# A block of two layers and attention: where the convolution taps stand among the key steps of the input projection

## The chip, the cores and the metric

The kernel runs on one core of a Trainium2 chip. The metric is the device time of one execution in microseconds (us); it was measured in three runs, and one more execution was profiled.

## The reference

The program computes two models one after the other on 512 tokens with 256 context tokens, all of width 1024: a two-layer block (a convolution branch beside a recurrence over 8 heads, then a SwiGLU network), and a block with attention and 32 experts. What matters here is the start of a layer, for x and for the context alike:

```python
ux = modulate(rmsnorm(x, norm1_g[l]), sh1, sc1) @ w_in[l]   # 23 column tiles of 128 or fewer
val, gate = jnp.split(ux[..., :1024], 2, axis=-1)           # tiles 0 to 7
z = dwconv(val * jax.nn.sigmoid(gate), conv_w) + conv_b     # 31 taps for each of 512 channels
u = dwconv(ux[..., 1024:], shift_w)                         # 3 taps, tiles 8 to 23
r, k, v, w_lo, a_lo, g_lo = jnp.split(u, ...)
kk = k * k_k
kk = kk / jnp.maximum(jnp.sqrt(jnp.sum(kk * kk, axis=-1, keepdims=True)), 1e-12)   # per head
```

## The kernel before

Each engine's program is written out by hand, in its own order, and the engines hold each other by semaphores. In the input projection of a layer (`input_projection`, one function of that name on each engine) they all walk through the same list, `input_steps`. It has the steps "product" n for n = 0 to 23, one column tile of the projection each (P0 to P23 below); behind each product from 16 on a "key" step, two for each of the four key tiles t (first half and second half); and "mod" and "turn" steps, small products for the next modulation. The order from P16 on is P16, key 0a, P17, key 0b, P18, key 1a, turn, mods, P19, key 1b, mods, P20, key 2a, P21, key 2b, turn, mods, P22, key 3a, P23, key 3b, mods, turn.

A product on TensorE (PE) is 24 matmuls over the 512 tokens and 24 over the context (three for each of 8 tiles, since operands are split into a high and a low part). It writes one of four pairs of PSUM banks, taken in turn by every product, head sum, mod and turn, so that one of these waits until the bank pair of the fourth before it has been read.

For P8 to P23, ScalarE (ACT) copies the product out of PSUM into `tmp` and, times the middle shift tap, into `work` (`raw_column`, L2420 to L2425). It then writes the high part of the weights two units ahead (`in_high`, L2648), for which the weight slot must have been loaded. VectorE (DVE) adds the other two shift taps (`token_shift`, L1622 and L1624) and writes the low part of the weights (`in_low`, L1663). Weights come in slots of 1024 KB through a ring of four; a slot is given free by the first matmul after its last use.

The first half of a key step for tile t is on DVE `start_key` (it scales tile t-1 by the finished norm, `scale_key` L1639, and multiplies the key tile, L1647) and on ACT the square of the result into the tile `rs` (L2463). The second half is on PE the head sum of `rs` (a product with `head_sum`, 128x512 and 128x256), on DVE `key_sum` (L1655, back into `rs`), and on ACT `key_norm`: logarithm (L2439) and exponential (L2443), each with a load of its table.

The convolution is on DVE alone, as 31 taps for each of four channel tiles: `conv_taps` issues the taps `first` to `last` of the table `CONV_ORDER`, one instruction each (L1610 the first of a tile, L1608 the others). A tap k on channel tile c waits for tap k-1 on the same tile. The last four taps stand at the end of the projection, behind the last `scale_key`. The others fill in between: 36 (`EARLY_TAPS`) behind products 3 to 7, and 84 inside `token_shift` of products 8 to 19, 7 in each. In the code of DVE these 7 come before the key step that follows the product:

```python
                late = len(CONV_ORDER) - 4 - EARLY_TAPS
                first, last = (EARLY_TAPS + late * min(m, TAP_COLUMNS) // TAP_COLUMNS for m in (n, n + 1))
                conv_taps(layer, first, last)
```

Of the kernel before, what the change touches and what calls it, by code (L numbers as in the profile page):

```python
# [20 lines left out]
TAPS = 31  # L21
# [50 lines left out]

def conv_order():

    order = [(k, c) for k in range(EARLY_TAPS // 2) for c in (0, 1)]
    order += [(k, c) for k in range(EARLY_TAPS // 2) for c in (2, 3)]
    order += [(k, c) for k in range(EARLY_TAPS // 2, TAPS) for c in range(4)]
    return [(k, c, order.index((k - 1, c)) if k else None) for k, c in order]


def raw_tile(n):


    return n - 8 if n < 16 else n - 4 if n < 20 else n - 12


def mod_groups(layer):

    return ([(0, q) for q in range(2, 6)] + [(1, 0), (1, 1)], [(1, q) for q in range(2, 6)] + [(2, 0), (2, 1)])[layer]


def in_unit(n):

    return n if n < 17 else n - 1
# [12 lines left out]
def input_steps(layer):  # L107

    n, turn = 0, None
    for slot in range(12):  # L110
        for h in range(((2,) * 8 + (3, 1) + (2,) * 2)[slot]):
            yield "product", n, h
            if n >= 16:
                yield "key", (n - 16) // 2, n % 2
            n += 1
        if turn:
            yield "turn", turn, None
            turn = None
        for i in range(2 * slot, 2 * slot + 2):
            yield "mod", mod_groups(layer)[i // 4], i % 4  # L120
        if i % 4 == 3:
            turn = mod_groups(layer)[i // 4]
    yield "turn", turn, None


EARLY_TAPS, TAP_COLUMNS = 36, 12
CONV_ORDER = conv_order()


# [101 lines left out]
def build(nc, ins, out):  # L231

    ctx = ExitStack()
    with ctx:
# [9 lines left out]
        def sem(name):  # L244
            return ctx.enter_context(nc.semaphore(name))
# [111 lines left out]
        def V(name, i=0, n=None):  # L357
            o, c = VOFF[name]
            return vec[:, o + i:o + i + (n or 1)]
# [19 lines left out]
        freed = {o: sem(f"product_read_{o}") for o in ("dve", "act")}  # L379
# [142 lines left out]
        def xs(t):  # L522
            return t[..., XO:XO + SEQ]

        def cs(t):
            return t[..., 0:CTX]
# [26 lines left out]
        def parts(with_ctx):  # L553

            return ((xs, 0), (cs, 1)) if with_ctx else ((xs, 0),)

        def grid(t, layer):

            return t.rearrange("p (c r) -> p r c", r=GRID_R) if layer == 1 else t.rearrange("p (r c) -> p r c", c=GRID_W)

        def natural(t):
            return t.rearrange("p (r c) -> p r c", c=GRID_W)

        def halves(j):

            return psum[:, 2 * j, :], psum[:, 2 * j + 1, 0:CTX]
# [956 lines left out]
        def _(dve):  # L1523
            w = Counts()
            banks = Results()
# [63 lines left out]
            def gated_value(layer, c):  # L1589
                j = banks.pair("dve")  # L1590
                dve.wait_ge(ready["dve"], banks.n["dve"])
                px, pc = halves(j)
                dve.wait_ge(freed["act"], gate_read[c])
                z = zp[:, c, GAP:GAP + W]
                tt(grid(xs(z), layer), natural(px), grid(xs(kk[:, c, :]), layer), ALU.mult)
                tt(cs(z), pc, cs(kk[:, c, :]), ALU.mult).then_inc(freed["dve"], 1)
                if c % 2:
                    dve.wait_ge(freed["dve"], banks.n["dve"])

            def conv_taps(layer, first, last):  # L1600

                for i in range(first, last):
                    k, c, before = CONV_ORDER[i]
                    a = 0 if layer == 0 else XO
                    src, acc, wt = zp[:, c, k + a:k + W], scr[:, c, a:W], V(f"conv_w{layer}", c * TAPS + k)
                    if k:
                        dve.wait_ge(conv_tap, w.seen[conv_tap] - i + before + 1)
                        ins = stt(ht[:, c, a:W] if k == TAPS - 1 else acc, src, wt, acc, ALU.mult, ALU.add)  # L1608
                    else:
                        ins = ts(acc, src, wt, V(f"conv_b{layer}", c), ALU.mult, ALU.add)  # L1610
                    ins.then_inc(conv_tap, 1)
                    w.skip(conv_tap)

            def token_shift(layer, n):
                banks.pair("act")
                dve.wait_ge(freed["act"], banks.n["act"])
                m = raw_tile(n + 8)
                rows = 64 if m in (12, 13) else 32 if m == 15 else P
                dst = (rkv[:, m, :] if m < 12 else lo[:, m - 12, :])[0:rows]
                src = tmp[0:rows, n % 2, :]  # L1620
                tap = lambda k: V(f"shift_w{layer}", 3 * m + k)[0:rows]
                stt(dst, src[:, 0:W], tap(0), dst, ALU.mult, ALU.add).then_inc(dve_chain, 1)  # L1622
                dve.wait_ge(dve_chain, w.next(dve_chain))
                stt(dst, src[:, 2:2 + W], tap(2), dst, ALU.mult, ALU.add).then_inc(raw_used, 1)  # L1624
                dve.wait_ge(raw_used, w.next(raw_used))
                u = in_unit(n + 8) + 2
                if n + 8 != 16 and u < 23:
                    in_low(layer, u)
                late = len(CONV_ORDER) - 4 - EARLY_TAPS
                first, last = (EARLY_TAPS + late * min(m, TAP_COLUMNS) // TAP_COLUMNS for m in (n, n + 1))  # L1630
                conv_taps(layer, first, last)

            gate_read = {}

            def scale_key(t):

                dve.wait_ge(gstd, w.next(gstd))
                for f, b in parts(True):
                    ins = tt(f(kk[:, t, :]), f(kk[:, t, :]), f(rs), ALU.mult)  # L1639
                ins.then_inc(dve_chain, 1)  # L1640
                dve.wait_ge(dve_chain, w.next(dve_chain))
# [17 lines left out]
            def in_low(layer, u):  # L1659

                dve.wait_ge(in_w_high, w.next(in_w_high))
                raw, low = in_weights(layer, u)[1]
                tt(low, raw, w_high[:, u % 2].bitcast(F32), ALU.subtract).then_inc(in_w_low, 1)  # L1663

            def input_projection(layer):
                for step, n, h in input_steps(layer):
                    if step == "key":
                        (key_sum if h else start_key)(layer, n)
                    elif step != "product":
                        banks.pair("act")  # L1670
                    elif n in (0, 1, 4, 5):
                        banks.pair("act")
                        gate_read[n // 4 * 2 + n % 2] = banks.n["act"]
                        in_low(layer, n + 2)
                        if n >= 3:
                            conv_taps(layer, EARLY_TAPS * (n - 3) // 5, EARLY_TAPS * (n - 2) // 5)
                    elif n < 8:
                        gated_value(layer, n // 4 * 2 + n % 2)
                        in_low(layer, n + 2)
                        if n >= 3:  # L1680
                            conv_taps(layer, EARLY_TAPS * (n - 3) // 5, EARLY_TAPS * (n - 2) // 5)
                    else:
                        token_shift(layer, n - 8)
                        if n == 19:
                            dve.memset(lo[64:65, 0:2, :], 1.0).then_inc(shifted, 1)
                scale_key(3)
                conv_taps(layer, len(CONV_ORDER) - 4, len(CONV_ORDER))
                dve.wait_ge(conv_tap, w.seen[conv_tap])
                dve.memset(mark, 0.0).then_inc(conv_out, 1)
                dve.wait_ge(conv_out, w.next(conv_out))  # L1690
# [345 lines left out]
            for layer in range(2):  # L2036
# [7 lines left out]
                if layer == 0:  # L2044
# [4 lines left out]
                    modulation(0, 0, 2)  # L2049
                norm(0, layer, True)  # L2050
                input_projection(layer)
                modulation(layer, 2, 6)
                modulation(layer + 1, 0, 2)
# [1017 lines left out]
```

## Time and profile before

| what | us |
|---|---|
| median of three runs | 4542.56 |
| lowest and highest of them | 4535.45, 4549.70 |
| the profiled execution's own time | 4540.72 |
| its span, first to last instruction | 4538.5 |
| input projection of layer 0, from P2 to the last tap | 85 to 344 |
| the same of layer 1 | 1501 to 1757 |
| busy share of the span: PE, DVE, ACT | 92%, 55%, 35% |

The profile is one execution, so its rows add up to 4540.72 us and not to the median. All times within it are from the span's start. The granted clock is given as a share of TensorE's full speed.

### The profile page before, as it was taken

What the parts mean: (1) busy time and instruction counts of PE and PEld (TensorE: products, weight loads), DVE (VectorE), ACT (ScalarE), POOL (GpSimd) and SP (SyncE); (2) the same over time, 40 slices, a digit from 0 to 9 for tenths busy, and PEclk for the clock granted to TensorE, in tenths of its full rate; (3) what the DMA queues carried; (4) which work ended last, traced back from release to release, by engine and by line L of the source; (5) the groups of instructions that cost most, each with busy time, mean ns of one, the idle gap of its engine ahead of it and who ended that gap; (6) DMA issues with size and microseconds to landing.
All of it is one profiled execution on the core that took longest, in us unless ns stands there. A gap on an engine that the chain in (4) does not pass through costs nothing.

```text
span 4538.5 us, 84941 instructions
## 1 busy us (share of the span) xinstructions
PE 4155.1 (92%) x37041; PEld 3207.8 (71%) x37041; DVE 2516.0 (55%) x3175; ACT 1568.7 (35%) x1923; POOL 118.8 (3%) x114
## 2 busy tenths in 40 slices
PE   6977998999999987999899969788699999999996
PEld 4857997588887866999488655443477777777774
DVE  4956775332222674776443320463477777777774
ACT  3243223100021334322200221253356666666662
POOL 0000000000000000000000000000200000000000
PEclk9988999999999998999999989899699999999997
DMA  6430000111122331000222225000499999999994
GB/s 246 154 116 12 4 4 31 56 65 57 65 68 86 145 135 61 4 4 4 84 94 98 96 73 188 25 1 29 170 336 353 356 354 352 359 356 355 352 357 143
DMA packets 115974, 663.46 MB, mean 146 GB/s; under 512 B 13632, under 2 KB 14656, under 8 KB 57696
## 3 DMA queue, kind: packets, MB, share of 16 engines
q1 hardware_dynamic: 102496, 610.68, 36.0%
q0 software_dynamic: 13168, 48.10, 3.9%
q8 instruction: 261, 4.28, 0.4%
q14 instruction: 49, 0.40, 0.0%
HBM read 637.62 MB, written 30.68 MB: 147 GB/s over the span
## 4 chain that ended last, share of the span: by engine, by line
PE 82%; DVE 11%; ACT 4%; DMA 2%; issue 2%; POOL 0%; SPq 0%; DVEq 0%; ACTq 0%; POOLq 0%
PE psum L791 54%; PE psum L1430 16%; PE psum L1456 5%; PE psum L1447 4%; DVE work L1608 2%; DVE xt L1812 1%; PE psum L1423 1%; DVE work L2138 1%; DMA ring<-stream 1%; PE psum L1404 1%; PE psum L1414 1%; DVE ring_parts L1663 0%; PE psum L1316 0%; POOL places L729 0%; DVE work L1624 0%
## 5 line engine op out<-in xcount | busy, mean ns | idle before, releaser
L791 PE MATMUL psum<-work 64*64 64x64 f32 (+3 forms) x12552 | 631.6, 239 | 66.2 <-ACT work L2747 21.8
L791 PE MATMUL psum<-ht_parts,ahead_parts 128*128 128x512 f32 (+1 forms) x2016 | 673.4, 350 | 0.6 <-DVE ht_parts L2005 0.6
L791 PEld LDWEIGHTS psum<-work 64*64 64x64 f32 (+2 forms) x12552 | 508.5, 138 | 145.2 <-issue 58.7
L791 PE MATMUL psum<-work_parts,ring_parts 128*128 128x512 f32 x1344 | 481.7, 359 | 0.0
L791 PE MATMUL psum<-work_parts,ahead_parts 128*128 128x512 f32 x1248 | 432.7, 359 | 10.3 <-ACT work_parts L2400 10.0
L791 PEld LDWEIGHTS psum<-ht_parts,ahead_parts 128*128 128x128 f32 (+1 forms) x2016 | 368.9, 186 | 60.7 <-issue 1.5
L791 PE MATMUL psum<-ht,ring 128*128 128x512 f32 (+1 forms) x832 | 315.4, 540 | 8.1 <-DVE ht L2154 6.1
L791 PEld LDWEIGHTS psum<-work_parts,ring_parts 128*128 128x128 f32 x1344 | 254.5, 189 | 40.0
L791 PE MATMUL psum<-xt_parts,ahead_parts 128*128 128x512 f32 (+5 forms) x768 | 265.1, 347 | 18.8 <-ACT xt_parts L2400 13.0
L791 PEld LDWEIGHTS psum<-ht,ring 128*128 128x128 f32 x832 | 157.8, 191 | 163.7 <-issue 150.9
L1430 PE MATMUL psum<-work_parts 128*128 128x512 f32 x1024 | 273.4, 393 | 0.0
L791 PEld LDWEIGHTS psum<-work_parts,ahead_parts 128*128 128x128 f32 x1248 | 234.5, 189 | 48.0 <-issue 11.5
L791 PE MATMUL psum<-xt_parts,ring_parts 128*128 128x512 f32 (+5 forms) x768 | 261.2, 342 | 0.0
L2242 DVE TENSOR_TENSOR ring_parts<-ring,work_parts 128x2048 fp32r<-128x2048 f32 x97 | 221.9, 2287 | 68.3 <-ACT work_parts L2809 68.3
L2809 ACT ACTIVATE work_parts<-ring 128x2048 fp32r<-128x2048 f32 x97 | 185.9, 1917 | 131.2 <-DMA ring<-w_in 120.7
L2242 DVE TENSOR_TENSOR ht_parts<-ht,work_parts 128x2048 fp32r<-128x2048 f32 x94 | 215.2, 2290 | 24.7 <-ACT work_parts L2809 24.5
L1430 PEld LDWEIGHTS psum<-work_parts 128*128 128x128 f32 x1024 | 192.6, 188 | 44.9 <-DVE ring_parts L2242 0.3
L2524 ACT ACTIVATE work<-psum 128x512 f32<-128x512 f32 x168 | 100.3, 597 | 344.7 <-PE psum L791 344.6
L1456 PE MATMUL psum<-ring,work 128*128 128x512 f32 x496 | 217.9, 592 | 0.0
L2601 ACT ACTIVATE work<-psum 128x512 f32<-128x512 f32 x44 | 26.3, 598 | 547.3 <-PE psum L791 547.3
L1430 PE MATMUL psum<-ring_parts,work_parts 128*128 128x512 f32 x768 | 211.3, 396 | 0.0
L1941 DVE SCALAR_TENSOR_TENSOR xt<-psum,mod,xt 128x512 f32<-128x512 f32 x40 | 32.8, 820 | 321.0 <-PE psum L791 321.0
(324 smaller groups left out, 7066.2 us busy)
## 6 DMA issues: line engine op xcount, KB each, us to landing
ring<-stream SPq DMA_DIRECT2D x192, 1024.0 KB, 4.9
ring<-w_in SPq DMA_DIRECT2D x192, 1024.0 KB, 6.7
ht<-w_in SPq DMA_DIRECT2D x64, 1024.0 KB, 6.4
ht<-w_out SPq DMA_DIRECT2D x64, 1024.0 KB, 7.4
ring<-w_out SPq DMA_DIRECT2D x64, 1024.0 KB, 7.0
xt<-xt_rows POOLq DMA_DIRECT2D x2, 3132.0 KB, 10.5
xt_rows<-xt POOLq DMA_DIRECT2D x1, 3132.0 KB, 14.3
xt_rows<-xt POOLq DMA_DIRECT2D x8, 391.5 KB, 3.2
```

The source lines that it names most:

```text
L791: mm = pe.matmul(*args, **kwargs)
L1404: mm = flush(pe.transpose(psum[:, 4 + k // 4, P * (k % 4):P * (k % 4) + P], x_tok[:, P * k:P * k + P], ident))
L1414: mm = flush(pe.transpose(psum[:, 4 + k // 4, P * (k % 4):P * (k % 4) + P], act[:, P * k:P * k + P], ident))
L1423: flush(pe.matmul(psum[:, b, :], one_hot, b_parts[:, 512 * b:512 * b + 512], start=True, stop=False))
L1430: mm = flush(pe.matmul(psum[:, b, :], x[:, k, :], wt[:, 512 * b:512 * b + 512], start=False, stop=(k == KT - 1 and x is x_low)))
L1447: flush(pe.matmul(psum[:, 6 + c, :], lhs[:, a], wt[:, f, 512 * c:512 * c + 512], start=(h == 0 and f == 0 and k == 0), stop=False))
L1456: mm = flush(pe.matmul(psum[:, 6 + c, :], e_act_high[:, P * (2 * h + f):P * (2 * h + f) + P], wt[:, f, 512 * c:512 * c + 512], start=False ...
L1608: ins = stt(ht[:, c, a:W] if k == TAPS - 1 else acc, src, wt, acc, ALU.mult, ALU.add)
L1812: ins = tt(dst[i % 2][:, g], ps, tri[:, g].to_broadcast([P, 4, 2, C]), ALU.mult)
L2242: tt(low_slots[k], raw_slots[k], highs[j % HIGHS].bitcast(F32), ALU.subtract).then_inc(low_ready, 1)
L2524: fn(dst, result(name, n, bank), ACT.Copy).then_inc(read_of[name], 1)
L2809: fn(highs[j % HIGHS], raw_slots[n % EXPERT_RING], ACT.Copy).then_inc(high_ready, 1)
```

## The change

Of the 124 taps of a layer none is added or left out; what moves is where they stand in the order of DVE. `TAPS_AT` says how many taps stand behind each place: indices 0 to 15 are the products 0 to 15, indices 16 to 22 the key steps 0a to 3a, each now behind the key step and not before it. So 5 taps stand behind product 2, 7 behind each of products 3 to 15, 3 behind each of key 0a, 0b, 1a and 1b, 4 behind each of key 2a, 2b and 3a, and as before 4 at the end. In `CONV_ORDER` the first ten taps are five of channel tile 0 and then five of tile 1, and the third and fourth tile begin at tap 40. Since taps of a tile now stand behind its gated value for tile 0 and 2 too, `gated_value` waits for its own result for every tile.

```diff
 def conv_order():
 
-    order = [(k, c) for k in range(EARLY_TAPS // 2) for c in (0, 1)]
+    first = [(k, 0) for k in range(5)] + [(k, 1) for k in range(5)]
+    order = first + [(k, c) for k in range(5, EARLY_TAPS // 2) for c in (0, 1)]
...
-EARLY_TAPS, TAP_COLUMNS = 36, 12
+EARLY_TAPS = 40
+TAPS_AT = [0, 0, 5] + [7] * 13 + [3] * 4 + [4] * 3 + [0]
...
-                if c % 2:
-                    dve.wait_ge(freed["dve"], banks.n["dve"])
+                dve.wait_ge(freed["dve"], banks.n["dve"])
...
             def input_projection(layer):
+                def taps_at(n):
+                    conv_taps(layer, sum(TAPS_AT[:n]), sum(TAPS_AT[:n + 1]))
+
                 for step, n, h in input_steps(layer):
                     if step == "key":
                         (key_sum if h else start_key)(layer, n)
-                    elif step != "product":
+                        taps_at(16 + 2 * n + h)
+                        continue
+                    if step != "product":
...
+                    if n < 16:
+                        taps_at(n)
```

PE, ACT, GpSimd and the DMA queues issue the same instructions in the same order as before. On DVE, the following is its order in layer 0 from the token shift of P16 (the rows 64x783) to `key_sum` of key 0b (rs<-psum), before. The rows work<-work,vec 128x783 x7 are taps, the TENSOR_SCALAR between them is `start_key`, and ring_parts is `in_low`.

```order
L1622 SCALAR_TENSOR_TENSOR work<-work,vec 64x783
L1624 SCALAR_TENSOR_TENSOR work<-work,vec 64x783
L1608 SCALAR_TENSOR_TENSOR work<-work,vec 128x783 x7
L1647 TENSOR_SCALAR work<-work,vec 128x783
L1622 SCALAR_TENSOR_TENSOR work<-work,vec 64x783
L1624 SCALAR_TENSOR_TENSOR work<-work,vec 64x783
L1663 TENSOR_TENSOR ring_parts<-ring,ahead_parts 128x8x128
L1608 SCALAR_TENSOR_TENSOR work<-work,vec 128x783 x7
L1655 TENSOR_SCALAR rs<-psum 128x512
```

The same stretch of DVE in the changed kernel, where the key multiplication is at L1646, the key sum at L1654 and a tap at L1610:

```order
L1624 SCALAR_TENSOR_TENSOR work<-work,vec 64x783
L1626 SCALAR_TENSOR_TENSOR work<-work,vec 64x783
L1646 TENSOR_SCALAR work<-work,vec 128x783
L1610 SCALAR_TENSOR_TENSOR work<-work,vec 128x783 x3
L1624 SCALAR_TENSOR_TENSOR work<-work,vec 64x783
L1626 SCALAR_TENSOR_TENSOR work<-work,vec 64x783
L1662 TENSOR_TENSOR ring_parts<-ring,ahead_parts 128x8x128
L1654 TENSOR_SCALAR rs<-psum 128x512
L1654 TENSOR_SCALAR rs<-psum 128x256
L1610 SCALAR_TENSOR_TENSOR work<-work,vec 128x783 x3
```

Seven taps before each half of key 0 have become three behind each. Near the start of the projection, DVE now has taps between the gated values of tiles 0 and 1 (work<-psum,work), which stood right behind `in_low` before:

```order
L1662 TENSOR_TENSOR ring_parts<-ring,ahead_parts 128x8x128
L1612 TENSOR_SCALAR work<-work,vec 128x783
L1610 SCALAR_TENSOR_TENSOR work<-work,vec 128x783 x4
L1598 TENSOR_TENSOR work<-psum,work 128x512
L1599 TENSOR_TENSOR work<-psum,work 128x256
```

The first two rows behind `in_low` are the five taps of channel tile 0 that moved forward.

## Rows read from the trace of the kernel before

**Rows 1.** Busy time in four stretches; PEclk is the granted clock.

```profile
84.00:239.00 155.00, 155.00 (x1057) 127.71 (x1050) 129.68 (x138) 38.46 (x76) 0.00 (x0) 1.00 0.43 163
239.00:340.00 101.00, 77.51 (x470) 57.14 (x468) 55.46 (x66) 44.00 (x75) 0.00 (x0) 0.87 0.32 115
1500.00:1655.00 155.00, 154.57 (x1051) 127.31 (x1044) 106.72 (x138) 48.37 (x76) 0.00 (x0) 1.00 0.43 163
1655.00:1753.00 98.00, 77.24 (x471) 57.22 (x469) 47.20 (x63) 49.23 (x73) 0.00 (x0) 0.88 0.33 119
```

**Rows 2.** Chain of work, layer 0: start us, us, what.

```profile
236.11 6.71 DVE work L1608 x7
...
262.55 4.80 DMA ring<-stream
...
284.62 6.62 DVE work L1608 x7
```

**Rows 3.** Chain of work, layer 1.

```profile
1652.37 4.73 DVE work L1608 x7
```

**Rows 4.** PE, instructions in order of time, layer 0; in brackets idle before, releaser.

```profile
244.29 2.93 PE L791 MATMUL psum<-rs,con 128*128 128x512 f32 x4 [4.77 <-ACT rs L2463]
...
261.98 0.39 PE L791 MATMUL psum<-xt_parts,ahead_parts 128*32 128x512 f32 x1 [2.01 <-ACT work L2425]
...
279.14 2.90 PE L791 MATMUL psum<-rs,con 128*128 128x512 f32 x4 [7.04 <-ACT mod L2363]
...
305.51 1.66 PE L791 MATMUL psum<-rs,con 128*128 128x512 f32 x4 [2.67 <-ACT rs L2463]
306.97 3.41 PE L791 MATMUL psum<-con,work 128*128 128x2 f32 x16
310.31 3.56 PE L791 MATMUL psum<-ring,work 128*32 128x256 f32 x32
313.80 0.50 PE L791 MATMUL psum<-xt_parts,ahead_parts 128*128 128x512 f32 x1
...
330.79 0.59 PE L791 MATMUL psum<-rs,con 128*128 128x512 f32 x1
```

**Rows 5.** PE in order of time, layer 1, the same places.

```profile
1658.57 1.22 PE L791 MATMUL psum<-rs,con 128*128 128x512 f32 x1 [2.78 <-ACT rs L2463]
...
1743.87 0.59 PE L791 MATMUL psum<-rs,con 128*128 128x512 f32 x1
```

**Rows 6.** DVE in order of time, layer 0: gated value 1, a column, a key step, P22.

```profile
102.15 0.69 DVE L1595 TENSOR_TENSOR work<-psum,work 128x512 f32<-128x512 f32 x1 [5.70 <-PE psum L791]
...
184.53 1.03 DVE L1622 SCALAR_TENSOR_TENSOR work<-work,vec 128x783 f32<-128x783 f32 x1
...
186.66 1.23 DVE L1663 TENSOR_TENSOR ring_parts<-ring,ahead_parts 128x1024 fp32r<-128x1024 f32 x1
187.81 6.70 DVE L1608 SCALAR_TENSOR_TENSOR work<-work,vec 128x783 f32<-128x783 f32 x7
...
276.34 1.02 DVE L1639 TENSOR_TENSOR work<-work,rs 128x512 f32<-128x512 f32 x2
277.40 0.63 DVE L1647 TENSOR_SCALAR work<-work,vec 128x783 f32<-128x783 f32 x1
...
324.44 1.04 DVE L1622 SCALAR_TENSOR_TENSOR work<-work,vec 128x783 f32<-128x783 f32 x1 [12.88 <-ACT work L2425]
```

**Rows 7.** ACT in order of time, layer 0: key norm, raw column, high weights, square.

```profile
256.96 0.94 ACT L2439 ACTIVATE rs<-rs 128x512 f32<-128x512 f32 x2 [8.79 <-DVE rs L1655]
...
260.05 0.58 ACT L2420 ACTIVATE work<-psum 128x512 f32<-128x512 f32 x1
...
261.36 0.48 ACT L2425 ACTIVATE work<-psum,vec 128x256 f32<-128x256 f32 x1
267.43 1.06 ACT L2648 ACTIVATE ahead_parts<-ring 128x1024 fp32r<-128x1024 f32 x1 [5.59 <-DMA ring<-stream]
278.06 0.85 ACT L2463 ACTIVATE rs<-work 128x783 f32<-128x783 f32 x1 [9.58 <-DVE work L1647]
```

More of the change, by code:

```diff
@@ L123, in input_steps @@
     yield "turn", turn, None
-EARLY_TAPS, TAP_COLUMNS = 36, 12
+EARLY_TAPS = 40
+TAPS_AT = [0, 0, 5] + [7] * 13 + [3] * 4 + [4] * 3 + [0]
+assert sum(TAPS_AT) == 4 * TAPS - 4 and sum(TAPS_AT[:8]) == EARLY_TAPS
 CONV_ORDER = conv_order()
@@ L1628, in token_shift @@
                     in_low(layer, u)
-                late = len(CONV_ORDER) - 4 - EARLY_TAPS
-                first, last = (EARLY_TAPS + late * min(m, TAP_COLUMNS) // TAP_COLUMNS for m in (n, n + 1))
-                conv_taps(layer, first, last)
             gate_read = {}
@@ L1668, in input_projection @@
                         (key_sum if h else start_key)(layer, n)
-                    elif step != "product":
+                        taps_at(16 + 2 * n + h)
+                        continue
+                    if step != "product":
                         banks.pair("act")
-                    elif n in (0, 1, 4, 5):
+                        continue
+                    if n in (0, 1, 4, 5):
                         banks.pair("act")
@@ L1674, in input_projection @@
                         in_low(layer, n + 2)
-                        if n >= 3:
-                            conv_taps(layer, EARLY_TAPS * (n - 3) // 5, EARLY_TAPS * (n - 2) // 5)
                     elif n < 8:
@@ L1679, in input_projection @@
                         in_low(layer, n + 2)
-                        if n >= 3:
-                            conv_taps(layer, EARLY_TAPS * (n - 3) // 5, EARLY_TAPS * (n - 2) // 5)
                     else:
```

## The prediction

> **What bounds the kernel now.** I read the two stretches that the change touches, in four windows first. Up to P17 PE is busy all the time at the full clock, 155 of 155 us in layer 0 and 154.57 in layer 1; in the stretch of the key steps it is busy 77.51 of 101 us and 77.24 of 98, and the granted clock falls to 0.87 and 0.88 [rows 1]. So PE loses about 23 and 21 us there by waiting, and something more by its clock. The chain of waits then says who makes it wait. In layer 0 it runs through four groups of seven taps, 6.6 to 6.7 us each, between the token shifts and the key steps (the first and the last are shown), and through one load of a weight slot [rows 2]; in layer 1 through four such groups of 4.6 to 4.7 us (the first is shown) [rows 3]. PE's own rows show where it lands: 4.77 us idle before the head sum of key 0, 2.01 before P19, 7.04 before the head sum of key 1, 2.67 before that of key 2 [rows 4].
>
> The mechanism is plain in the code and in these rows. PE is in order, so the head sum of a key blocks the product behind it. It needs ACT's square, which needs `start_key`, and that stands behind 7 taps on DVE. Likewise `key_sum` stands behind 7 taps, ACT's key norm waits for it, and behind the key norm stands ACT's raw column of P18, whose bank P19 needs. P19's first matmul frees the slot whose load the next high weights need.
>
> **What one step costs.** From the rows of DVE: token shift 2.13 us (184.53 to 186.66), low weights 1.15, a tap 0.95 (seven in 6.6); scale 1.06 and key multiplication 0.64 [rows 6]. In layer 1 a tap is 0.67 (4.7 for seven) [rows 3]. From ACT: square 0.8, key norm 3.1 (256.96 to 260.05), raw column 1.8, high weights 1.07 [rows 7]. From PE at full clock: two products in 16.99 us (313.80 to 330.79), so 8.5 each; a head sum 1.45 (305.51 to 306.97) [rows 4]. The turn and the mods, at the lower clock 3.34 and 3.49 in these rows, I take at 1.85 and 1.9, half of that and a little over. The load of a slot ends 5.4 us after the matmul that frees the last one (261.98 to 267.35) [rows 2, 4].
>
> **Layer 0, replayed with the taps behind the key steps.** Up to P16 nothing on the path changes: DVE's column of 9.9 us stays as it was, with seven taps.
>
> Key 0: the token shift of P16 ends at 236.1, where now the seven taps begin [rows 2]. The key multiplication follows at once, the square is ready near 237.7, and P17 ends on PE only at 239.5 (244.29 less its idle of 4.77) [rows 4]. The head sum starts then: 4.8 us earlier, no gap. It ends at 240.9, P18 at 249.4, turn and mods at 253.2.
>
> P19: raw column of P17 239.5 to 241.4, then three taps are long done (239.6), token shift and low weights until 244.7, `key_sum` until 245.8, key norm until 248.9. The raw column of P18 starts with the end of P18 at 249.4 and is read out at 251.3, before PE comes to P19 at 253.2. The gap of 2.01 is gone; P19 is 8.8 us earlier than 261.98.
>
> Key 1: P19 starts at 253.2, its freed slot is loaded at 258.6, high weights 259.7, low weights 260.9, scale and multiplication 262.6, square 263.4, the turn's copy 0.2, so the head sum starts at 263.8. PE was done with P19 at 261.7: a gap of 2.1 stays where 7.04 was. 15.3 us earlier than 279.14.
>
> P20 and P21 run from 267.2 to 284.2. `key_sum` of key 1 comes at 272, long before P21's bank is needed. Square 2 is ready near 283.5 (raw column of P20 277.6, token shift, low weights, scale, multiplication, square: 5.8 more), so key 2 has no gap: head sum 284.2, 21.3 earlier than 305.51. Turn and mods until 289.5. P22 needs the bank of this head sum: raw column of P21 until 286.1, four taps done at 286.5, token shift and low weights 289.8, `key_sum` 290.9. P22 starts at 291.0, a new gap of 1.5, where it started at 313.80: 22.8 earlier. P22 and P23 take 17, and nothing holds key 3. What is behind the head sum of key 3 (330.79) is as before. **Layer 0 gains 22.8 us if PE keeps its full clock.**
>
> **Layer 1,** the same way with taps of 0.67, the raw column near 2.6 and P17 ending at 1655.8 (1658.57 less 2.78) [rows 5]: head sum 0 at once (2.78 earlier), P19 at 1669.4, head sum 1 at 1680.0 after a gap of 2, P20 at 1683.4, head sum 2 at 1701.1 after a gap of 0.7, P22 at 1708.1 after a gap of 1.9, head sum 3 at 1725.1 in place of 1743.87 [rows 5]. **It gains 18.8.** As a bound from the other side, the 28 taps taken out of the chain are 26.6 us in layer 0 and 18.7 in layer 1 [rows 2, 3].
>
> **The clock.** The head sum after the gap of 4.77 took 2.4 (244.29 to the next product at 246.7) and not 1.45, the turn and the mods after the gap of 2.67 took 6.8 and not 3.7 [rows 4], and the stretch was granted 0.87 [rows 1]. In the replay gaps of 0.7 to 2.1 stay, two in layer 0 and three in layer 1. If none is followed by a spell at 1.2 GHz, the gain is 41.6 as summed; if each is followed by one that costs as much as in these rows, 1 to 3 us, it is 31 to 37. The row before P19 has a gap of that size, 2.01, and the sum can't say which way it goes, so I take off 2 us for each layer. **Sum: 41.6 - 4 = 37.6 us.**
>
> On this the Trainium skill has a rule: TensorE: Matmul & The Clock Gate, in the part on the clock gate, says that the throttled state is the default and that activity releases it. By that rule only the long gaps would cost clock, and since they go the gain would be near the 41.6. This trace agrees for the gap of 4.77 and shows the full clock through the 155 busy us ahead of it.
>
> **Edits costed at nothing.** The 24 taps that now stand behind key steps are hidden by waits of DVE for ACT's raw columns: in the replay DVE still waits before every token shift from P17 on but that of P21, which the four taps before it delay by 0.4. Without that cover they would cost 24 x 0.95 + 24 x 0.67 = 39 us. The five taps behind P2 take 4.9 us, within the 5.70 that DVE idles before the gated value of tile 1 [rows 6]; taps of one tile in a row wait for each other, which a pair of dependent instructions shows as 1.07 in place of 0.95 apart (184.53 to 186.66 for two) [rows 6], so 0.5 more for these five: still inside. Were they late by all of it, `in_low` of P5 would have a whole product in hand. The additional wait in `gated_value` is for DVE's own last instruction and is 0.1 us at most in the same pair, twice a layer. All other engines issue the same order. The convolution's last four taps and all behind them follow the key norm of key 3 as before.
>
> **The rivals.** (a) The taps behind keys 2a, 2b and 3a come onto the path. Before, there were none from P20 on, so this part is new load: 12 x 0.95 + 12 x 0.67 = 19.4 us. DVE's idle there speaks against it, 12.88 us before the token shift of P22 [rows 6], though it shrinks by the taps. It would leave 18 us: 4524. (b) All 24 are on the path: then only four taps of each layer are saved, 3.8 + 2.7 = 6.5 us, 4536, which counts as no change. Key 0 speaks against it in the replay: its three taps end at 239.6, and the raw column that DVE waits for next is ready at 241.4. (c) The gain is real but is given back, because what follows waits for something that does not move, the spill of xt or the weights of the recurrence. 4543. Against it: the queues move 115 GB/s here against 163 ahead [rows 1], and each load is released by a matmul that itself moves. (d) Slower: PE is busy without a break for longer, and its clock is granted at the lower level through the key stretches. Eight products of 8.5 us in each layer would cost 136 us more, which gives 4542.6 - 41.6 + 136 = 4637; it decides from 41 us of PE work at half speed on. The 155 us of unbroken work at 1.00 [rows 1] speak against it.
>
> **How the numbers follow.** The chances: forecast 0.80, (a) 0.09, (b) 0.04, (c) 0.04, (d) 0.03. The profiled execution was 4540.72, the median of the three runs 4542.56; the gain is the same for both: 4540.7 - 37.6 = 4503.1, and against the median 4542.6 - 37.6 = 4505.0, which I predict. The forecast's own range is a gain of 31 to 44, 4499 to 4512. The range given is 4495 to 4525: it takes in (a), a run-to-run spread of some us (the three runs lie 14 apart) and, below, a gain of the 28 taps in both layers (45.3). Under 0.3%, 13.6 us, a measurement of this kernel can't tell a difference. Faster by more: forecast and (a), 0.89; within: (b) and (c), 0.08; slower: 0.03.
>
> **What would show it.** In the changed trace: no idle of PE before head sum 0 and P19; 2 us before head sum 1 on the high weights' load; none or little before head sum 2; 1 to 2 us before P22, on `key_sum`; head sum 3 near 308 and 1725 - 22.8 = 1702; the granted clock of the key stretches over 0.93; no taps in the chain between a token shift and a key step. The prediction is wrong if taps stand in the chain still, if PE's gap before head sum 1 is more than 4 us, or if the recurrence begins no earlier.

## The result and the profile after

The changed kernel takes 4509.99 us (median of four runs, 4508.09 to 4518.09) against 4542.8 before (four runs: the three of the table above and the profiled one): 0.9931 of the time, 95% interval 0.9912 to 0.9951. That is 32.8 us faster, where 37.6 were forecast; the time lies in the range given. The profiled execution has a span of 4505.9 us, 32.6 less than that of before.

Busy time of the changed kernel, in the first stretch of [rows 1], then in its key steps of layer 0 and of layer 1 (columns as there):

```profile
84.00:239.00 155.00, 155.00 (x1044) 127.85 (x1043) 133.45 (x141) 38.96 (x75) 0.00 (x0) 1.00 0.43 162
239.00:322.00 83.00, 71.21 (x476) 55.18 (x474) 55.37 (x64) 42.50 (x73) 0.00 (x0) 0.94 0.41 147
...
1639.00:1723.00 84.00, 71.18 (x475) 54.17 (x472) 46.23 (x61) 49.39 (x74) 0.00 (x0) 0.93 0.39 138
```

The key stretches are 83 and 84 us long in place of 101 and 98. PE idles 12 to 13 us in them and not 21 to 24, and the granted clock is 0.94 and 0.93 in place of 0.87 and 0.88 [rows 1].

PE of the changed kernel in order of time, layer 0, which answers to [rows 4]:

```profile
237.48 1.45 PE L794 MATMUL psum<-rs,con 128*128 128x512 f32 x4
238.58 0.58 PE L794 MATMUL psum<-xt_parts,ahead_parts 128*128 128x512 f32 x1
...
263.31 2.15 PE L794 MATMUL psum<-rs,con 128*128 128x512 f32 x4 [3.87 <-ACT mod L2366]
265.40 2.94 PE L794 MATMUL psum<-ring,work 128*32 128x256 f32 x32
268.27 0.49 PE L794 MATMUL psum<-xt_parts,ahead_parts 128*128 128x512 f32 x1
...
292.06 0.46 PE L794 MATMUL psum<-xt_parts,ahead_parts 128*128 128x512 f32 x1 [1.82 <-DVE rs L1654]
...
309.00 0.59 PE L794 MATMUL psum<-rs,con 128*128 128x512 f32 x1
```

The head sum of key 0 follows P17 with no gap. P19 has none either. Before the head sum of key 1 a gap of 3.87 us is left of 7.04, and a new one of 1.82 stands before P22. The program began this stretch 1.84 us earlier by chance of its start-up (gated value 0 on DVE at 91.85, at 93.69 before), so head sum 3, at 309.00 and 330.79 before [rows 4], is 19.95 us nearer to that point. The same in layer 1, its PE waits of the key stretch:

```profile
PE psum L794 <- ACT work L2360: 6.5, 1, 6.5
PE psum L794 <- ACT mod L2366: 4.1, 1, 4.1
PE psum L794 <- DVE rs L1654: 1.8, 1, 1.8
PE psum L794 <- ACT rs L2466: 0.3, 1, 0.3
```

The first of these stands behind head sum 3 and was there before; the second is the gap before head sum 1, the third that before P22.

The chain of work of the changed kernel where that gap ends, layer 0:

```profile
251.44 6.69 DMA ring<-stream
...
258.22 1.07 ACT ahead_parts L2651
...
259.38 1.23 DVE ring_parts L1662
260.61 0.95 DVE work L1638 x2
...
261.58 0.64 DVE work L1646
...
263.00 0.17 ACT mod L2366
```

No tap stands in this piece. What it waits for is the load of the weight slot, 6.69 us and not 4.80 [rows 2], and the two weight steps behind it.

Taps are not gone from the chain altogether. In layer 0 it runs, ahead of P22, through the four taps behind key 2a; in layer 1 no taps stand in it from key 0 to P22. The same chain, layer 0:

```profile
283.83 3.87 DVE work L1610 x4
...
287.70 0.96 DVE work L1624
...
290.89 1.03 DVE rs L1654 x2
...
292.06 17.13 PE psum L794 x96
```

DVE of the changed kernel at the two places where its taps come closest to something (the four taps behind key 2a, and the first five):

```profile
95.49 4.24 DVE L1610 SCALAR_TENSOR_TENSOR work<-work,vec 128x783 f32<-128x783 f32 x4
100.26 0.69 DVE L1598 TENSOR_TENSOR work<-psum,work 128x512 f32<-128x512 f32 x1 [0.53 <-PE psum L794]
...
283.83 3.87 DVE L1610 SCALAR_TENSOR_TENSOR work<-work,vec 128x783 f32<-128x783 f32 x4
287.62 1.03 DVE L1624 SCALAR_TENSOR_TENSOR work<-work,vec 128x783 f32<-128x783 f32 x1
```

The first five are done 0.53 us before the gated value of tile 1 is wanted. The four behind key 2a end as the token shift of P21 begins, without idle between them.

**Where the time is.** Five pieces of the two traces give the 32.6 us of the span. The start-up gave 1.84, layer 0 19.95. From the end of layer 0's taps (344.38 before, 322.53 after) to the first low weights of layer 1 (1499.95 and 1483.99) the changed kernel takes 5.9 us more. Layer 1, from there to head sum 3 (1743.87 and 1712.67), gives 15.24, and the rest of the program 1.4. The 5.9 us are the part that the prediction had not foreseen. The first and the last piece are chance as far as the traces show: the second trace of before (before_again, below) spends 3.6 us less in the rest of the program than the first (2791.1 and 2794.7), with the same kernel. So the two layers are surer than the total.

### The profile page after: what moved, and what is told of

Its sections match the earlier page's. It is cut to its first block, busy times and chain, and to the rows that moved or that the text cites. A ratio compares the mean times of both kernels' runs of the same rounds, so it can differ in the third digit from the quotient of the medians.

```text
span 4505.9 us, 84943 instructions
## 1 busy us (share of the span) xinstructions
PE 4146.4 (92%) x37041; PEld 3204.2 (71%) x37041; DVE 2518.4 (56%) x3175; ACT 1570.2 (35%) x1923; POOL 118.8 (3%) x114
## 4 chain that ended last, share of the span: by engine, by line
PE 85%; DVE 8%; ACT 3%; DMA 2%; issue 1%; POOL 0%; SPq 0%; DVEq 0%; ACTq 0%; POOLq 0%
PE psum L794 57%; PE psum L1433 16%; PE psum L1459 5%; PE psum L1450 4%; DVE xt L1815 1%; DVE work L2141 1%; PE psum L1426 1%; DMA ring<-stream 1%; PE psum L1407 1%; PE psum L1417 1%; POOL places L732 0%; PE psum L1319 0%; ACT work L2750 0%; DMA sum_rows<-work 0%; DVE ht L1561 0%
## 5 line engine op out<-in xcount | busy, mean ns | idle before, releaser
L1944 DVE SCALAR_TENSOR_TENSOR xt<-psum,mod,xt 128x512 f32<-128x512 f32 x40 | 32.8, 820 | 323.0 <-PE psum L794 323.0
```

## The experiments

All edits are against the changed kernel, but for `before_again`. The table has, for each profiled execution, the stretch of layer 0 (gated value 0 to head sum 3), the stretch between the layers (behind the last tap of layer 0, in `delayed` behind its fills, to the first low weights of layer 1), PE's busy time in it, how much of this is at the lower clock (1.2 GHz), and the stretch of layer 1 (first low weights to head sum 3), in us. The ratios are to runs of the kernel before that were made along with each kernel, whose medians were 4542.8 (for changed), 4539.19 (again, behind_only, spread_ahead, no_key_taps) and 4541.18 (the others):

| kernel | median | ratio to before, 95% | layer 0 | between | PE busy between | of it at the lower clock | layer 1 |
|---|---|---|---|---|---|---|---|
| before | 4542.8 | | 237.10 | 1155.6 | 1091.1 | 34.1 | 243.92 |
| before_again | 4540.99 | 1.0002 (0.9991 to 1.0012) | 237.20 | 1155.5 | 1091.1 | 34.1 | 244.02 |
| changed | 4509.99 | 0.9931 (0.9912 to 0.9951) | 217.15 | 1161.5 | 1097.3 | 47.4 | 228.68 |
| again | 4509.11 | 0.993 (0.9913 to 0.9946) | 217.53 | 1161.3 | 1097.0 | 47.5 | 228.51 |
| behind_only | 4513.76 | 0.9942 (0.9925 to 0.9958) | 218.96 | 1161.3 | 1099.4 | 51.5 | 227.89 |
| spread_ahead | 4530.07 | 0.998 (0.9969 to 0.999) | 233.89 | 1156.0 | 1091.4 | 34.2 | 239.11 |
| no_key_taps | 4505.90 | 0.9933 (0.9916 to 0.9949) | 217.06 | 1159.1 | 1094.2 | 39.7 | 228.27 |
| delayed | 4512.09 | 0.9936 (0.9922 to 0.9949) | 217.25 | 1158.2 | 1094.1 | 40.9 | 227.75 |
| late_weights | 4497.12 | 0.9907 (0.9892 to 0.9922) | 213.04 | 1155.5 | 1091.1 | 34.3 | 222.80 |
| late_weights_2 | 4492.62 | 0.9895 (0.9881 to 0.9908) | 210.07 | 1161.6 | 1097.3 | 48.0 | 221.65 |

### behind_only: the place alone

```diff
-    first = [(k, 0) for k in range(5)] + [(k, 1) for k in range(5)]
-    order = first + [(k, c) for k in range(5, EARLY_TAPS // 2) for c in (0, 1)]
+    order = [(k, c) for k in range(EARLY_TAPS // 2) for c in (0, 1)]
...
-EARLY_TAPS = 40
-TAPS_AT = [0, 0, 5] + [7] * 13 + [3] * 4 + [4] * 3 + [0]
+EARLY_TAPS = 36
+TAPS_AT = [0, 0, 0, 7, 7, 7, 7, 8] + [7] * 8 + [7] * 4 + [0] * 4
```

> Only the place is changed: the counts and the order of taps are those of before (36 by product 7, seven with each of products 8 to 19), but for products 16 to 19 the seven stand behind the key step and not ahead of it. Theory (the place is what counts; taps behind a key step are hidden by the waits for raw columns even when there are seven): head sum 3 of layer 0 within 2 us of where the changed kernel has it, 309.0, and the time within 5 us of 4510. Rival (the spread over more key steps and the five early taps matter): seven taps behind key 0a and 0b delay the next token shift, 2 to 4 us in each of four places are lost, and the time is 4520 to 4530.

Layer 0 is 18.1 us shorter than before and layer 1 16.0, against 19.95 and 15.24 for the whole change. The median is 4513.76, 3.8 us over the changed kernel. Head sum 3 stands at 313.07, 4 us later than 309.0, where within 2 us was expected; but this execution had also begun later (gated value 0 at 94.11), and set against that point it is 1.8 us. So the place carries the gain. The spread, with the five early taps, gives 1.8 us in layer 0, where seven taps of 0.95 us behind a key step leave a gap of 1.3 before head sum 2, and nothing in layer 1, where a tap is 0.67. PE's waits of the key stretch, layer 0, of behind_only:

```profile
PE psum L793 <- ACT work L2359: 5.8, 1, 5.8
PE psum L793 <- ACT mod L2365: 3.9, 1, 3.9
PE psum L793 <- ACT rs L2465: 1.3, 1, 1.3
PE psum L793 <- DVE rs L1653: 1.1, 1, 1.1
```

### spread_ahead: the counts alone

```diff
-                        (key_sum if h else start_key)(layer, n)
                         taps_at(16 + 2 * n + h)
+                        (key_sum if h else start_key)(layer, n)
```

> The other part alone: the counts and the order of the changed kernel (5 behind product 2, 3 and 4 with the seven key steps), but the taps of a key step stand ahead of it, as before. Theory: they are on the chain, 24 in place of 28, and those of keys 2a, 2b and 3a are new there; head sum 3 of layer 0 is only 5 to 9 us earlier than 330.8, the time is 4525 to 4535. Rival (fewer taps in each place is what brings the gain): most of the gain is kept, 4512 to 4520.

Layer 0 gains 3.2 us, less than the 5 to 9 expected, and layer 1 4.8, 8.0 in all; the median is 4530.07, within the range expected and 9.1 below that of before in the same set of runs. The taps are on the chain of work again, three or four at a time, those of the keys from 2a on included (spread_ahead, layer 0):

```profile
245.53 2.84 DVE work L1610 x3
...
264.72 2.84 DVE work L1610 x3
...
290.48 3.78 DVE work L1610 x4
...
301.92 3.78 DVE work L1610 x4
...
321.09 3.87 DVE work L1610 x4
```

Three or four taps ahead of a key step cost nearly what seven did in fewer places. The rival that fewer taps in each place bring the gain is out.

### no_key_taps: what the hidden taps still cost

```diff
-TAPS_AT = [0, 0, 5] + [7] * 13 + [3] * 4 + [4] * 3 + [0]
+TAPS_AT = [0, 0, 5] + [7] * 13 + [0] * 8
+CONV_K = TAPS - 6
```

> Leaves part of the computation out: the convolution has 25 of its 31 taps, and the 24 that stood behind the key steps are gone; all else stands as in the changed kernel. Theory (they are fully hidden): the same time as the changed kernel within 3 us, head sum 3 of layer 0 near 309. Rival (they still cost, above all those behind keys 2a, 2b and 3a, where DVE's token shift of P21 follows without a wait): up to 19 us less, by 12 taps of 0.95 and 12 of 0.67.

The run leaves out six of the 31 taps of each channel tile, and with them all taps behind the key steps. Layer 0 takes 217.06 us without the taps and 217.15 with them, layer 1 228.27 and 228.68. The 24 taps, 22.8 and 16 us of work, cost 0.1 and 0.4 us, no more than two traces of the changed kernel differ by (0.4 and 0.2). The median, 4505.90 against 4509.99, is 4.1 us less where within 3 was expected; it differs by the stretch between (1159.1 against 1161.5) and by what one run differs from the next. The gap before head sum 1, 4.0 us here, isn't made by taps at all. That before P22 in layer 0 is 1.6 us in place of 1.8, so the four taps that stand in the chain there cost about 0.2 us.

### again and before_again: the 5.9 us between the layers

Both kernels unchanged, for a second trace.

> The changed kernel once more, for a second trace. Between the end of the projection of layer 0 and P2 of layer 1 the first trace of the changed kernel is 5.9 us longer than that of before (the lead is 21.85 us at the last tap and 15.96 at P2 of layer 1). Theory 1: that is the granted clock of the work in between, which differs from one execution to the next, and is no cost of the change: this stretch, 1162.8 us in the first trace of the changed kernel and 1156.9 before, will be off 1162.8 here by some us either way. Rival: it is a cost of the change (another clock phase set by the earlier arrival): the stretch will be 1162.8 again within 1 us.

> The kernel before once more, for a second trace. A second run of the changed kernel had its stretch from the last tap of layer 0 to P2 of layer 1 at 1161.3 us, as the first (1161.5), against 1155.6 in the one trace of before: my theory that this is chance from run to run has fallen. Theory now: each kernel has its own fixed length there, set by where the granted clock falls; before will have 1155.6 within 1 us. Rival: before varies, and its one trace was lucky: 1158 to 1162.

The first theory fell: the changed kernel had 1161.3 us again. The second held: before has 1155.5. In two traces of each kernel it isn't chance from run to run. The stretch between in the first trace of before (columns as in [rows 1]):

```profile
344.40:1500.00 1155.60, 1091.11 (x14448) 932.06 (x14452) 509.90 (x912) 235.57 (x400) 4.87 (x9) 0.97 0.13 44
```

The same in the first trace of the changed kernel:

```profile
322.50:1484.00 1161.50, 1097.25 (x14448) 936.83 (x14452) 509.72 (x912) 235.56 (x400) 4.87 (x9) 0.97 0.13 43
```

And in that of again:

```profile
323.50:1484.90 1161.40, 1097.04 (x14448) 937.45 (x14452) 509.80 (x912) 235.56 (x400) 4.87 (x9) 0.97 0.13 43
```

PE has the same 14448 matmuls in all of them, DVE and ACT the same busy time to 0.2 us. The matmuls alone are 6 us longer. What makes the same matmuls longer is the clock. Of PE's busy time in this stretch 34.1 us are at the lower of its two levels before, and 47.4 in the changed kernel. At half speed the 13.3 us more hold 6.7 us of full-speed work, which so costs 6.7 us more, against 6.1 measured; over all ten traces the table's two columns agree in this way within 0.8 us. An example is the end of the recurrence, where PE comes back after 11.5 us idle (at 781.43 before, at 761.48 in the changed kernel). Before, its clock is at the lower level until 784.70 and at the full one in the output projection behind it:

```profile
774.46:784.70 10.24, 3.27 (x5) 1.85 (x6) 7.18 (x12) 6.33 (x12) 0.00 (x0) 0.50 0.00 0
...
795.00:814.00 19.00, 17.84 (x50) 8.81 (x51) 3.53 (x7) 0.00 (x0) 0.00 (x0) 1.00 0.30 110
```

In the changed kernel it rises at 765.83, and falls once more, from 782.90 to 786.31, just before the same output projection, in an idle of PE of 1.16 us that before has too, without a fall:

```profile
752.18:765.83 13.65, 4.35 (x6) 2.19 (x7) 9.06 (x15) 8.65 (x17) 0.00 (x0) 0.50 0.00 0
782.90:786.31 3.41, 2.85 (x4) 1.33 (x5) 0.46 (x2) 0.00 (x0) 0.00 (x0) 0.50 0.00 0
```

### delayed: the same stretch, reached later

```diff
                 dve.wait_ge(conv_tap, w.seen[conv_tap])
+                if layer == 0:
+                    dve.memset(tmp, 0.0).then_inc(dve_chain, 1)
+                    dve.wait_ge(dve_chain, w.next(dve_chain))
+                    dve.memset(tmp, 0.0).then_inc(dve_chain, 1)
+                    dve.wait_ge(dve_chain, w.next(dve_chain))
```

> The changed kernel, with two fills of 1.37 us each added on VectorE behind the last tap of layer 0, where PE waits for it: 2.8 us more on the path. PE has 14448 matmuls in the stretch from there to P2 of layer 1 in all traces, busy 1097 us in both traces of the changed kernel and 1091 us in those of before and of spread_ahead. Theory: the extra 6 us come from where in its own rhythm the granted clock meets PE's waits of this stretch, and not from what the change did; the arrival 2.8 us later meets it as before did. From the end of the fills to P2 of layer 1 it takes 1156 and not 1161.5, and the kernel is 3 us faster than the changed kernel in spite of the added work. Rival: the stretch stays at 1161 and the kernel is 2.8 us slower.

Half a hit. From the end of the fills the stretch takes 1158.2 us and not 1161.5, with PE busy 1094.1: the same work, reached later, is 3.3 us shorter, in one trace. But it isn't the 1156 expected, and the fills put 3.5 us on the path (head sum 3 to the end of the stretch 17.05 in place of 13.53), so the kernel is not faster: 4512.09, 2.1 us over the changed one, which the measurement can't tell from it.

The table says without the fills that the length belongs to no part of the change: late_weights, whose projection is even shorter, has 1155.5 there, and late_weights_2 1161.6. Nor is it the time of arrival counted from the start of the span: the last tap ends at 322.5, 322.9 and 323.5 us in the changed kernel, no_key_taps and again, and the stretch takes 1161.5, 1159.1 and 1161.3. What sorts most of the traces is where the kernel meets the fall of the clock behind head sum 3. It falls 6.67 to 6.77 us behind the start of that head sum in before, before_again and late_weights (1155.5 and 1155.6), 6.64 behind it in no_key_taps (1159.1), and 5.49 to 6.38 in behind_only, again, changed and late_weights_2 (1161.3 to 1161.6). spread_ahead (1156.0), where it falls at the start of that head sum, stands outside this order, and so does delayed, whose work behind the head sum is another. That is a pattern in the traces; no run set this distance by itself.

### late_weights and late_weights_2: a step further

The square of key 1 needs nothing of the weight slot whose load it waits for; it only stands behind `in_high` and `in_low` in the order of ACT and DVE. The first edit puts these two behind (ACT's behind the copies of the mods):

```diff
+LATE_LOW = (16, 18)
...
                     taps_at(16 + 2 * n + h)
+                    if (n, h) == (1, 0):
+                        in_low(layer, 19)
...
-                if n + 8 != 16 and u < 23:
+                if n + 8 not in LATE_LOW and u < 23:
...
+                    if step == "product" and n == 19:
+                        next_high(18)
...
-                        next_high(n)
+                        if n != 18:
+                            next_high(n)
```

> A step further than the changed kernel: ACT's high weights for P20 stand behind its copies of the mods, and DVE's low weights for P20 behind key 1a and its taps, so that the square of key 1 no longer waits for the load of a weight slot that starts with P19. Theory (PE's gap of 3.9 and 4.1 us before head sum 1 is the load, 6.7 to 6.9 us, and the two weight steps behind it): head sum 1 follows P19 without a gap, and with the slow clock behind the gap gone the projection is 5 us shorter in each layer; 4500 within 7. Rival (the square is then late for another reason, or P20 waits for its low weights instead): 4507 to 4511.

The time is 4497.12, 13 us less than the changed kernel. Layer 0 is 4.1 us shorter and layer 1 5.9, where 5 were expected for each; in layer 1 the wait before head sum 2 grows from 0.3 to 1.0 us. PE's waits of late_weights, layer 0:

```profile
PE psum L795 <- ACT work L2363: 5.7, 1, 5.7
PE psum L795 <- DVE rs L1655: 1.8, 1, 1.8
```

The wait before head sum 1 is gone and its head sum takes 1.45 us. About 6 us of the 13 are the stretch between, 1155.5, which is luck of the clock and not work that the edit took away.

The second edit adds the change of the table for the gap before P22:

```diff
-TAPS_AT = [0, 0, 5] + [7] * 13 + [3] * 4 + [4] * 3 + [0]
+TAPS_AT = [0, 0, 5] + [7] * 13 + [3, 3, 7, 3, 0, 4, 4, 0]
...
+LATE_LOW = (16, 18, 21)
...
                         (key_sum if h else start_key)(layer, n)
+                        if (n, h) == (2, 1):
+                            in_low(layer, 22)
```

> late_weights, with the four taps behind key 2a moved behind key 1a (seven there), and the low weights for P23 behind the key sum of key 2. Theory: the key sum of key 2 comes 2 us earlier, and the gap of 1.8 us before P22 in each layer goes: 3 to 4 us less than late_weights. Rival: seven taps behind key 1a delay the low weights for P20, and nothing is gained over late_weights.

4492.62 us, 1.05% under before. Over late_weights layer 0 is 3.0 us shorter and layer 1 1.2; the wait before P22 in layer 0 is 0.4 us in place of 1.8, and the other 1.6 us there are the clock: behind that wait of 1.8 it had fallen to the lower level in late_weights (288.9 to 292.4), and here it stays at the full one up to head sum 3 (late_weights_2, layer 0):

```profile
PE psum L795 <- ACT work L2365: 5.7, 1, 5.7
PE psum L795 <- DVE work L2063: 2.9, 1, 2.9
PE psum L795 <- DVE rs L1655: 0.4, 1, 0.4
```

Its stretch between is the long one. The medians of the two, 4.5 us apart with intervals that overlap, don't show which is faster; the traces show it for the projections.

## Why the prediction was right, point by point

**The bound.** Right. The taps ahead of the key steps were on the chain, and place alone gives nearly the whole gain (behind_only). With the taps behind, one group of four is left in the chain, that behind key 2a in layer 0, and it costs 0.2 us (no_key_taps). The replay had this delay, at 0.4 us, but the prediction also named "taps stand in the chain still" as a sign of being wrong. By the letter that sign came; by its cost it says nothing against the mechanism.

**Key 0 and P19.** Right: no gap before either. The replay had P19 8.8 us earlier than 261.98; measured from gated value 0 it is 9.3 earlier (250.85 less 91.85 against 261.98 less 93.69).

**Key 1.** The mechanism was right, one term too small. The replay took the load of the slot at the 4.8 us of [rows 2] and a gap of 2.1; the load took 6.69 and 6.95 us and the gap was 3.87 and 4.13. That is the step of the prediction that was mis-sized, and a gap of more than 4 us was one of its signs of being wrong: layer 1 is over it by 0.1, and layer 0 in the trace of again by 0.2. DMA moved 336 GB/s at a share of 0.87 all through it (changed kernel, the load and the waits behind it in layer 0):

```profile
251.40:258.20 6.80, 6.80 (x38) 3.95 (x37) 0.00 (x0) 0.00 (x0) 0.00 (x0) 1.00 0.87 336
```

That is 2.3 MB, more than two slots of 1024 KB. P19's load is the third of three that are issued one behind the other, here within 4.11 us and in the kernel before within 6.16. Here:

```profile
247.67 4.11 SPq L650 DMA_DIRECT2D ring<-stream  x3
```

Before:

```profile
256.72 6.16 SPq L647 DMA_DIRECT2D ring<-stream  x3
```

In the changed kernel P19 follows the mods without a pause, so that the two loads ahead are still under way when P19's is asked for. Before, P19 came 2 us late, and they had had that time: in the 4.9 us of its load (262.5 to 267.4) DMA moved 324 GB/s, which is 1.6 MB and not 2.3. Taking away one wait put part of it on the next. That it is this was read from the traces; no run made the loads ahead smaller.

**Key 2 and P22.** Right: no gap before head sum 2 in layer 0, 0.33 in layer 1 (0.7 in the replay); before P22 1.8 in both, where the replay had 1.5 and 1.9.

**The clock.** I took off 2 us a layer for spells at 1.2 GHz. The head sum behind the gap took 2.1 us in layer 0 and the mods behind it 2.9, against 1.45 and 1.9: 1.6 us. In layer 1 they took 2.8 and 2.7, 2.2 us. Nothing was lost at P22 in either. So the term was right in size. Whether a gap of 1.8 us costs clock is not settled by its length: late_weights had the same gap before P22 in layer 0 and lost 1.6 us behind it. On the Trainium skill's rule (TensorE: Matmul & The Clock Gate, in the part on the clock gate) that activity releases the throttle: the spell of lower clock in the turn and the mods of key 2 did go with the gap of 2.67 us ahead of it, as it has it, and one stayed in layer 0 behind the gap of 3.87. The 41.6 us that I worked out with it were out of reach because of the load, which kept that gap long.

**The sum.** Forecast 20.8 + 16.8 = 37.6; measured in the projections 19.95 + 15.24 = 35.2. The load alone was 1.9 and 2.1 us longer than the replay had it. P19, 0.5 and 0.4 us earlier than in the replay, the shorter gap before head sum 2 in layer 1 and the smaller loss by the clock in layer 0 (0.4 each) gave about 1.6 of these back. From 35.2 to the 32.6 of the span it is the stretch between, -5.9, with the start-up, +1.8, and the rest of the program, +1.4. The sum had the first of these three at nothing without a reason: it took the work between the layers as fixed. The other two are chance and were luck for the forecast. Head sum 3 of layer 0 came at 309.0, near the 308 named. That of layer 1 was named at 1702 and came at 1712.7: most of the 10.7 us are the clock (3.8), which that figure leaves out, the load (4.0) and the stretch between (5.9), less what came early.

**Edits costed at nothing.** Right: 0.1 and 0.4 us for the 24 taps, within what two traces of a kernel differ by, and 0.53 us to spare behind the first five, for which the replay had 5.70 less 5.4.

**The rivals.** (a) taps behind keys 2a to 3a on the path: the four behind key 2a do, in layer 0, and hold the token shift of P21, but at 0.2 us of the 19.4 that the rival had. (b) is out by the same run. (c) is out as it was put, since neither the spill nor a weight load took the gain back; but 5.9 of 35 us were given back between the layers, by the clock, which no rival had. (d) did not occur in the key stretches, where the clock rose to 0.94.

**What stays open:** why the clock's spells between the layers fall differently in one kernel than in another; delayed shows only that moving the work ahead of the stretch moves them. And whether the 1.8 us of the spread in layer 0 is worth its code: the medians of behind_only and of the changed kernel don't differ clearly.

## What to carry to other kernels

In an engine's program written out by hand, filler work belongs behind the instruction that another engine waits for, not ahead of it: here 28 taps a layer, moved from ahead of four key steps to behind them, were worth 34 us in the two layers together (behind_only), and the rest of the change about 1 us more. Where the taps stay ahead of the key steps, the counts and the order of the change were worth 8 us (spread_ahead). Then look at the next thing that stands ahead of that instruction without being needed by it; here it was a weight step that waited for a load, and moving it past gave another 4 to 6 us a layer. And compare stretch by stretch, from one fixed event to the next: a median of 33 us hid a gain of 35 and a loss of 6, the latter in work that the edit never touched (and 3 us that were chance).

## What the runs showed of the hardware

Work that an edit leaves alone can change its length by 6 us in 1156: the same 14448 matmuls took PE 1091.1 to 1099.4 us in ten traces, by how much of them stood at the lower clock (34.1 to 51.5 us). Two traces of one kernel agreed within 0.2 us, in each of two kernels; kernels that differ only ahead of the stretch were up to 8.3 apart. A difference of a tenth of a per cent between two versions of this kernel may be no more than that.

Taps of one channel tile in a row, each waiting for the last, start 1.07 us apart (4.24 for four), and taps of four tiles in turn 0.95 (3.87 for four): a wait for the instruction directly ahead costs 0.1 us on DVE.
